# Routed experts of a hybrid decoder layer: units of four 32-token pieces in place of 128-token blocks

## What is computed

```python
scores = jax.nn.sigmoid((t @ w_router).astype(F32))
...
_, eidx = lax.top_k(sel, TOP_K)
wts = jnp.take_along_axis(scores, eidx, axis=1)
wts = wts / jnp.sum(wts, axis=-1, keepdims=True) * ROUTED_SCALE
...
hid = jax.nn.silu(xblk @ w1[e]) * (xblk @ w3[e])
return hid @ w2[e]
...
routed = jnp.zeros((T, Dm), F32).at[tok_buf].add(yb.reshape(cap, Dm).astype(F32) * w_buf[:, None])
shared = (jax.nn.silu(t @ ws1) * (t @ ws3)) @ ws2
```

## Time and profile before

| what | value |
|---|---|
| median of 3 runs | 1860.33 us (1853.07 to 1861.6) |
| the profiled execution, its own time | 1858.06 us |
| its span, first to last instruction | 1855.5 us |
| TensorE busy | 1667.8 us (90%) |
| VectorE busy | 977.8 us (53%) |
| GpSimd busy | 625.5 us (34%) |
| moved by DMA | 367.72 MB, mean 198 GB/s |

### The profile page before, as it was taken

One profiled execution on the slowest core, in us unless ns is written; L12 is line 12 of the kernel. 1 busy time (PEld: TensorE's weight loads), 2 busy tenths in 40 slices (PEclk: granted clock), 3 DMA queues, 4 the chain that ended last, 5 costly groups with the idle time before them and its releaser, 6 DMA issues.

```text
span 1855.5 us, 20259 instructions
## 1 busy us (share of the span) xinstructions
PE 1667.8 (90%) x4917; PEld 806.8 (43%) x4918; DVE 977.8 (53%) x2247; ACT 232.2 (13%) x390; POOL 625.5 (34%) x680
## 2 busy tenths in 40 slices
PE   4989999998999997798899999999999999999960
PEld 2444545445455463343344444444444444444420
DVE  0177878988988947473333333333333333333327
ACT  1112123122122122111000000000000000000003
POOL 0001101101001000065455555555555555555541
PEclk8999999999999995798999999999999999999985
DMA  9973000001000071375299797998989978998944
GB/s 335 336 252 137 34 36 25 34 25 37 34 5 35 36 257 34 86 212 135 96 365 300 223 366 240 293 370 301 300 286 276 348 218 274 339 351 296 336 77 188
DMA packets 102662, 367.72 MB, mean 198 GB/s; under 512 B 21411, under 2 KB 37703, under 8 KB 77613
## 3 DMA queue, kind: packets, MB, share of 16 engines
q1 hardware_dynamic: 72949, 298.70, 43.5%
q0 software_dynamic: 29664, 68.51, 16.7%
HBM read 322.17 MB, written 64.72 MB: 209 GB/s over the span
## 4 chain that ended last, share of the span: by engine, by line
PE 60%; DVE 16%; DMA 10%; issue 7%; SPq 3%; POOL 2%; ACT 1%; DVEq 0%; POOLq 0%; ACTq 0%
PE U L744 26%; PE R L759 13%; PE U L586 10%; DVE cv L1075 7%; PE R L632 5%; DMA acc_rows<-W,slot_cur 4%; DMA acc_rows<-xr,slot_cur 3%; POOL slot_tab L1517 2%; SPq L319 2%; DMA W<-in_w_ada 1%; PE T L603 1%; PE T L750 1%; PE R L624 1%; DMA x_t<-h_rows,tok_cur 1%; PE U L682 1%
## 5 line engine op out<-in xcount | busy, mean ns | idle before, releaser
L586 PE MATMUL U<-W,hT 128*128 128x512 f32 x864 | 390.5, 607 | 1.2 <-issue 1.2
L744 PE MATMUL U<-W,cat 128*128 (+1 forms) x720 | 326.0, 607 | 22.1 <-issue 14.4
L759 PE MATMUL R<-W,glu 128*128 (+1 forms) x728 | 329.0, 595 | 11.2 <-issue 9.8
L744 PE MATMUL U<-W,hT 128*128 (+1 forms) x736 | 326.4, 597 | 1.7 <-issue 1.6
L1075 DVE SCALAR_TENSOR_TENSOR cv<-win,cw,cv 128x128 f32<-128x128 f32 x960 | 269.8, 363 | 2.0
L586 PEld LDWEIGHTS U<-W,hT 128*128 128x128 f32 x864 | 165.1, 196 | 191.0 <-issue 191.0
L759 PEld LDWEIGHTS R<-W,glu 128*128 128x128 f32 x728 | 139.0, 191 | 185.5 <-issue 183.8
L744 PEld LDWEIGHTS U<-W,cat 128*128 128x128 f32 x720 | 136.5, 195 | 181.9 <-issue 179.6
L744 PEld LDWEIGHTS U<-W,hT 128*128 128x128 f32 x736 | 137.5, 192 | 158.9 <-issue 158.8
L1531 POOL DMA_INDIRECT x_t<-h_rows,tok_cur x168 | 171.0, 1018 | 78.0 <-issue 39.5
L1531 POOL DMA_INDIRECT W<-h_rows,tok_cur x168 | 170.2, 1013 | 76.6 <-issue 38.6
(11 more groups left out here) (242 smaller groups left out, 1228.2 us busy)
## 6 DMA issues: line engine op xcount, KB each, us to landing
W<-in_w SPq DMA_DIRECT2D x192, 1024.0 KB, 9.0
W<-in_w_ada SPq DMA_DIRECT2D x24, 1024.0 KB, 9.5
W<-in_w_in SPq DMA_DIRECT2D x6, 2048.0 KB, 19.9
x_rows<-xr SPq DMA_DIRECT2D x9, 512.0 KB, 2.6
h_rows<-xr SPq DMA_DIRECT2D x9, 512.0 KB, 2.6
x_t<-in_x_prompt SPq DMA_DIRECT2D x8, 512.0 KB
W<-in_w_out SPq DMA_DIRECT2D x1, 4096.0 KB, 18.8
xr<-in_x_prompt SPq DMA_DIRECT2D x8, 512.0 KB
```

The source lines that it names most:

```text
L586: last = mm(U[BANK[g]][:, :], hT[:, k, :], w_in[:, k, 512 * g:512 * g + 512], start=k == 0, stop=k == KT - 1)
L744: last = mm(U[1][:, :], xgT[z][:, k, :], w13[:, :, k, :], start=k == 0, stop=k == KT - 1)
L759: last = mm(R[:, 512 * half:512 * half + 512], hidT[:, f, :], weights[:, at:at + 512], start=f == 0, stop=f == FT - 1)
```

## The change

- **Pieces and units.** `RANKS` holds a number of 32-token pieces for each rank of the experts by token count (10 for the largest, 1 for the seven smallest; 225 in all, enough for these inputs). `groups()` puts ranks together so that four pieces make a unit of one or two experts, and `even_order` spreads them: 57 units, known when the program is built. 29 units hold one expert; 11 hold two pieces of each of two experts; 17 hold three pieces of one and one of another.
- **Products on column tiles.** `tiles_of` cuts a unit's 128 columns at 4, 2 and 1 pieces. A unit of one expert issues the products as before; a unit of 2 + 2 issues each twice on 64 columns; a unit of 3 + 1 issues each three times, on 64, 32 and 32 columns.

```diff
+            def tiles_of(parts):
+                for at, width, weights in parts:
+                    while width:
+                        step = next(x for x in (4, 2, 1) if x <= width and at % x == 0)
+                        yield slice(32 * at, 32 * at + 32 * step), weights
+                        at, width = at + step, width - step
+
+            def up(n, parts, z):
                 pe.wait_ge(xgT_ready, n + 1)
-                w13 = weights[:, 0:KT * 2 * DE].rearrange("p (x k n) -> p x k n", x=2, k=KT)
                 for k in range(KT):
-                    last = mm(U[1][:, :], xgT[z][:, k, :], w13[:, :, k, :], start=k == 0, stop=k == KT - 1)
+                    for cols, weights in tiles_of(parts):
+                        w13 = weights[:, 0:KT * 2 * DE].rearrange("p (x k n) -> p x k n", x=2, k=KT)
+                        last = mm(U[1][cols, :], xgT[z][:, k, cols], w13[:, :, k, :], start=k == 0, stop=k == KT - 1)
                 last.then_inc(h_done, 1)
...
+            for u in range(NU):
+                for s in sorted({s for s, q in QUARTERS[4 * u:4 * u + 4] if q == 0}):
+                    pe.wait_ge(ring_in[s % RING], 48 * (s // RING + 1))
+                up(NT + u, parts_of(u), (NT + u) % 2)
+                if u > 0:
+                    down(NT + u - 1, parts_of(u - 1))
+                hidden_trans(NT + u)
+            down(NT + NU - 1, parts_of(NU - 1))
```

`down` is cut in the same way. The experts are loaded in the order of the plan, from a row of expert numbers; the `up` part of a load waits for `h_done` of the last unit of the expert four before, the `down` part for its `y_done`:

```diff
+            def load_in_line(s):
+                e = sp.value_load(line_i[0:1, s:s + 1], min_val=0, max_val=NE - 1)
+                if s >= RING:
+                    sp.wait_ge(h_done, NT + last_unit[s - RING] + 1)
+                load_up(e, s % RING, 0)
+                load_up(e, s % RING, 1)
+                if s >= RING:
+                    sp.wait_ge(y_done, NT + last_unit[s - RING] + 1)
+                load_down(e, s % RING)
```

- **Two tables.** The two experts of a unit may share a token, so results go to one of two tables in `acc_rows`, by the parity of the expert's place in line. The second is filled with zeros in the mixer (five transfers of 1 MB). At the end both come back, and TensorE adds them with the identity as weights:

```diff
+            for i in range(TP):
+                pe.wait_ge(acc_in[i // 2], 16 + 64)
+                pe.wait_ge(gated, floor(i - 1))
+                for half in (slice(0, 512), slice(512, 1024)):
+                    for x in (acc_t[i], odd_t[i]):
+                        last = mm((X, R)[i % 2][:, half], ident[:, :], x[:, half], start=x is acc_t[i], stop=x is odd_t[i])
+                last.then_inc(sum_done, 1)
```

More of the change, by code:

```diff
@@ L36, with groups, units_of, even_order @@
 TOKENS = SEQ + NS
[L37 to L41, removed]
+RANKS = (10, 8, 7, 7, 6, 6, 6, 6, 6, 5, 5, 5, 5, 5, 5, 5) + (4,) * 10 + (3,) * 19 + (2,) * 12 + (1,) * 7
+def groups():
+    rest = [[x for x in range(NE) if RANKS[x] % 4 == r] for r in range(4)]
+    made = [[x] for x in rest[0]]
+    for big, small in ((3, 1), (2, 2)):
+        while len(rest[big]) > (big == small) and rest[small]:
+            made.append([rest[big].pop(0), rest[small].pop()])
+    while rest[3]:
+        made.append([rest[3].pop(0) for _ in range(min(4, len(rest[3])))])
+    assert not rest[1] and not rest[2]
+    return made
+def units_of(group):
+    return -(-sum(RANKS[x] for x in group) // 4)
+def even_order(made):
+    pace = sum(units_of(x) for x in made) / NE
+    order, units, experts = [], 0, 0
+    while made:
+        best = min(made, key=lambda x: abs(units + units_of(x) - pace * (experts + len(x))))
+        made.remove(best)
+        order.append(best)
+        units, experts = units + units_of(best), experts + len(best)
+    return order
+GROUPS = even_order(groups())
+LINE = tuple(x for group in GROUPS for x in group)
+QUARTERS = ()
+for group in GROUPS:
+    own = [(LINE.index(x), q) for x in group for q in range(RANKS[x])]
+    own += [(own[-1][0], own[-1][1] + 1 + q) for q in range(-len(own) % 4)]
+    QUARTERS += tuple(own)
+NU = len(QUARTERS) // 4
+assert NU % 2 == 1 and all(len({x for x, _ in QUARTERS[4 * u:4 * u + 4]}) < 3 for u in range(NU))
+TABLE = 10 * P
+CAPS = tuple(32 * sum(x == s for x, _ in QUARTERS) for s in range(NE))
+ROUNDS = -(-(TOKENS - min(CAPS)) // P)
+LCAP = -(-(max(CAPS) + P * ROUNDS) // 32) * 32
 RING = 4
@@ new lines, in _ @@
+            down(0, shw_all)
+            positions(TP, pick_s[:, :], NT)
+            hidden_trans(1)
+            rank_products()
+            for n in range(2, NT):
+                up(n, shw_all, n % 2)
+                down(n - 1, shw_all)
+                hidden_trans(n)
+                if n == 2:
+                    spread_lists()
+                if n == 3:
+                    pe.wait_ge(rounds_posed, 1)
+                    mm(U[0][0:1, 0:NE], rounds_c[0:NE, :], ident[0:NE, 0:NE], start=True, stop=True).then_inc(rounds_posed, 1)
@@ new lines, in _, with parts_of @@
+            down(NT - 1, shw_all)
+            def parts_of(u):
+                parts = []
+                for at in range(4):
+                    s = QUARTERS[4 * u + at][0]
+                    if parts and parts[-1][0] == s:
+                        parts[-1][2] += 1
+                    else:
+                        parts.append([s, at, 1])
+                return [(at, width, ring[:, s % RING, :]) for s, at, width in parts]
+            for u in range(NU):
[5 more added lines that the diff above has]
+                hidden_trans(NT + u)
@@ L1180, in body @@
                     conv(0, TAPS[0])
+                if late:
+                    place(m - 2, pick, i - 1)
                 if route:
@@ L1420, in _, with routed @@
+            for n in range(4, NT - 1):
+                shared(n)
             shared(NT - 1)
             shared_y(NT - 1)
-            dve.wait_ge(blkrow_ready, 1)
-            dve.wait_ge(h2_stored, 16 * NT)
-            last = dve.value_load(pend_i[0:1, NE:], min_val=MINPAIR - 1, max_val=MAXPAIR - 1)
             dve.wait_ge(ysh_stored, 16 * NT)
-            def routed(g, r, first=False):
+            def routed(g, r, first=False, last=False):
                 b = 2 * g + r
-                if r == 0:
+                if r == 0 and not last:
```

604 lines of the change are left out of this document (330 added, 274 removed).

## The result

The change takes 1862.66 us (median; 1856.93 to 1871.97), the kernel before, run beside it, 1859.34 us (1853.07 to 1862.5). The ratio is 1.0026, 95% interval 1.0015 to 1.0037: 3 to 7 us slower, within the half per cent that the prediction called no change. The forecast was 1834 us. The profiled execution has a span of 1861.0 us, 5.5 more than before, and it is this difference that is taken apart here.

The account below looks back on a forecast made before the run. The prediction took TensorE in the routed stage as the bound, with the DMA engines close to full. From 1858 us: routed stage -44, mixer +5, shared stage +4, end +11, giving 1834 us, range 1805 to 1875.

Parts of the forecast that it names:

- Fewer blocks, equal widths: Routed stage: 82 blocks become 57 units; equal-width products run side by side, 10.53 us per one-expert unit, 11.2 per 2 + 2.
- rival C: Routed stage: products on 64 columns don't pair, a 2 + 2 unit's `up` takes 13.7 us; 1947 us in all, chance 0.04.
- Change of width: Routed stage, TensorE: 64- and 32-column products don't overlap; a change there and back costs 0.34 us, a 3 + 1 unit 24.9.
- Rival B: Routed stage: the change of width costs twice, four changes per step in place of two; 1903 us in all, chance 0.12.
- rival A: Routed stage: products of two widths run side by side, so the transfers bound; 1692 us in all, chance 0.27.
- Transfers under it: Routed stage: 244 MB at 357 GB/s take 684 us, hidden under TensorE's 860, with four slots for expert weights.
- Gaps at the experts' first units: Routed stage: listed as a sign that the forecast is wrong; no size given.
- The other 8 us of the stage: Routed stage: of 27 us of short waits and register loads 8 stay, making 852 us of TensorE work 860.
- Mixer: Mixer stage: list work moved here adds 5 us (-10 to +15), from two more TensorE products per tile.
- I book 0 for VectorE: Mixer: VectorE's list operations and the norm leaving the path ahead of the convolution's end count 0, -2 to +2 us per tile.
- Shared stage: Shared blocks: list wait and a slow block go, about 8 us of VectorE work and 4 of indirect reads come; +4 us.
- End: End of kernel: two tables read back, sums over TensorE and a third GpSimd operation add 11 us (+5 to +20).

Follow-up runs that it names:

- e4: The change with each divided unit's products reordered, in `up` and each half of `down` first all on 64 columns, then all on 32: 1820.88 us.
- e1: The change with a fifth slot in the weight ring, the place of the shared weights, free after the shared blocks: 1798.61 us.
- e8: The change with VectorE's first norm of the next tile put back ahead of the convolution's last taps, as before the change: 1879.68 us.
- e7: The change without reading and summing the second table at the end, so results of experts at odd places are left out: 1858.04 us.
- e2: The change with units of 3 + 1 pieces cut into four products of 32 columns in place of 64, 32 and 32: 1674.83 us.
- e5: The change with both four 32-column products for 3 + 1 units and a fifth weight slot: 1629.29 us, ratio 0.8759 to the kernel before.

## Why the prediction was wrong

- **Fewer blocks, equal widths: right.** A 2 + 2 unit's `up` takes 7.09 us; rival C (13.7) is out.
- **Change of width: right, a little large.** "There and back is 0.34 us"; e4 shows 0.27. A 3 + 1 unit takes 24.1 us, 15.9 + 7.9 + 0.3, against 24.9, a 2 + 2 unit 10.8 against 11.2: 18 us less on TensorE. Rival B (two more changes per step) is out, and rival A too: no unit of 3 + 1 in the change has an `up` under 15.5 us. The Trainium skill's page "TensorEngine Tiling (Array Packing)", section "Key Properties", says that a change of mode drains the engine. The runs agree for 64 to 32 columns (an `up` of 3 + 1 takes 15.95 us, grouped 14.07), which the trace of before couldn't show. The Trainium skill's page "TensorE: Matmul & The Clock Gate", section "The mechanism", has products overlap whose masks name different columns. Here that shows between equal widths alone (7.09 us for two of 64 and 7.07 for four of 32, against 7.03 for one of 128).
- **Transfers under it: the step that failed.** "With four slots the next experts are under way while a unit runs": the sum compared 684 us of transfers with 860, called them hidden, and put waits for weights at nothing. Gaps at the experts' first units stood among the signs of being wrong, without a price. The mean was right, DMA share 0.78 for a forecast 0.75; but a ring isn't drawn at its mean. A unit of 3 + 1 holds two of the four slots for its 24 us and the `up` after it, and in that time SyncE lets out little or nothing (28 us after 1049.84); what comes then comes late, or in a bunch. That is 45.5 us of waits and 16.4 us of slow products behind them, 62 together, and e1 gets 59.5 of them back in the stage (918.3 to 858.8). In the kernel before, where a block holds one slot, no `up` of the routed stage but the first waited more than 1.3 us.
- **The other 8 us of the stage: right, in part by luck.** "Of the 27 us I keep 8": with the weights on time, in e1, TensorE is idle for 9 us of the stage (858.8 less 849.5). It is busy there for some 16 us more than the units' prices as measured add up to (29 x 10.53 + 11 x 10.8 + 17 x 24.1 = 834), which makes up for the shorter products; where these 16 lie was not followed up. So e1's 858.8 meets the 860 closer than its parts deserve.
- **Mixer: wrong sign.** The products' +5 isn't shown by itself; without the norm's move the mixer is 6 us longer than before (e8). "I book 0 for VectorE" was wrong: the norm's move was seen and not priced. The wait that it shortens, TensorE's for the convolution's mean, was to be read in the list of waits of the kernel before, in the mixer, and the step should have started there:

```profile
PE T L603 <- DVE cv L1075: 19.0, 7, 3.5
```

- **Shared stage: -7 for +4.** What comes was priced well: `hidden_trans` of block 1 waits 7.49 us for VectorE, for the 8 forecast,

```profile
787.42 0.70 PE L834 MATMUL T<-ident,sg 128*128 128x128 f32 x2 [7.49 <-DVE sg L1439]
```

  and the fourth block starts 63.1 us after the first, 8.6 later than before, where 12 were booked in all. What goes was counted too low: from the fourth block to the first routed `up` it took 90.0 us and takes 74.2, 15.7 less, where 8.2 were booked (the wait for the list and one slow block). Before, one block more was late and slow there: it started at 853.58, 13.3 us after the one ahead of it, and its `up` took 8.73 us. No run took this stage apart; these are readings of the two traces, and that the list work was the cause is not shown.
- **End: +9.5 for +11**, right as a size; e7 bears out about 4 us of its parts, the others weren't tried.

That 1862.66 us lies within the forecast's own range (1805 to 1875) is luck: the mixer and the shared blocks came out 16 and 11 us better than forecast and paid nearly half of the routed stage's 58. The time is that of none of the rivals. A's time, 1692 us, was to be had, but by not mixing widths (e2, 1675).

## What to carry to other kernels

Compare a ring of buffers with the longest stretch in which one user holds its slots, not transfers' total with compute's total. What the issuing queue stands in sum is no sign: SyncE stood 624 us for a `down` in the kernel before, 697 in the change and 637 in e1, where next to nothing was late. Go from each late product back to the load that it waited for, and read when that went out and how long it took: landed in 4.8 us, it went out late; landed in 14 to 19, it stood behind others. On TensorE cut divided tiles into equal widths, even if that means more products: four on 32 columns took 7.07 us where 64 + 32 + 32 took 15.95. And where several limits lie close together, lift them in turn and read after each which one has come up: room (e1), TensorE (e2), then the DMA engines (e5).

## What was not expected of the hardware

- Eight waits of 4.3 to 8.0 us on TensorE each cost another 1.5 to 2.7 us in the `up` after it (two of 0.75 and 1.52 us cost none): an `up` of 7.03 us took 9.65 after 4.34 us idle, one of 15.95 took 18.39 after 5.67 and 17.77 after 8.01. The window around three of the waits has a mean granted clock of 0.88, part of it at the lower level; a stretch with few of them has 1.00, the upper level of 2.4 GHz (the change, 1025 to 1125 and 1140 to 1540):

```profile
1025.00:1125.00 100.00, 83.02 (x225) 22.70 (x223) 19.31 (x20) 1.92 (x5) 31.85 (x37) 0.88 0.73 254
1140.00:1540.00 400.00, 392.11 (x1119) 103.95 (x1116) 91.73 (x92) 8.45 (x23) 139.23 (x162) 1.00 0.75 252
```

- In e5 the DMA engines ran at 360 GB/s for 685 us on end, and a load's landing went from 10.5 to 19.7 us (median), yet TensorE waited less for weights than in the change, where they landed sooner. A landing time in a full queue says how much stands ahead of a load; whether it comes late, only the product that needs it shows.
